# A hybrid conv / state-space / Fourier block on one core: context quarters turned early, C tables turned ahead of B, state tables loaded ahead of the first conv weights

## Chip, cores and metric

One Trainium2 chip, one of its cores. The metric is the device time of the launch in microseconds (us), the median of repeated runs. The profile is of one more execution.

## What is computed

One layer (DEPTH = 1) of a parallel-branch block on 512 latent tokens and 256 context tokens, width 2048, fp32. Cut to what matters here:

```python
mod_x = silu(c) @ w_ada + b_ada          # shift, scale, gate of the latent tokens
mod_c = silu(c_ctx) @ w_ada + b_ada      # the same for the context
h_x = rmsnorm(x, g_pre) * (1 + sc_x) + sh_x
h_c = rmsnorm(ctx, g_pre) * (1 + sc_c) + sh_c
parts_x = split(h_x @ w_in)
u_c = h_c @ w_in[:, U_OFF:U_OFF + W_SSM] # the context is only read by the SSM
# branch B: for both directions
a, bb = zoh(lam, log_dt, b)              # state matrices
cr, ci = scan(u_c, a, bb, None)
xr, xi = scan(u_x, a, bb, h0=last context state)
y = readout(xr, xi, c_re, c_im)
# then conv branch, GLU, Fourier branch, three gated merges, w_out, RMSNorm, residual
```

## The kernel before

Activations are kept transposed: a tile of 128 channels is on the partitions, the tokens are the columns. Every large product is a sum of three fp32r products. ScalarE (ACT) makes the rounded high part of a weight tile (`whi`), VectorE (DVE) or GpSimd (POOL) the remainder (`wlo`); the activations are held as pairs (`hxh`, `hxl` for the latent, `hch`, `hcl` for the context). A unit of weights is 128 x 1024 floats, 512 KB, in one of four slots `wslot`, and is numbered through the program: units 0 to 7 are the first half of U's columns, 8 to 15 the second half (`u_turn`), 16 to 79 the conv turns, and so on. TensorE (PE) counts units done in `w_used`; SyncE (SP) may load unit u when u-3 are done, ACT may convert unit u when u-1 are done.

**Prologue.** SP streams 32 MB of `w_ada` through four `ring` buffers (64 loads of 512 KB, `ada_unit`); PE multiplies each by the two conditioning vectors (`ada(n)`, L631) and frees it (`ada_used`). The model width is taken in four quarters q. For quarter q PE turns the modulation rows into columns (`cols(q)`, L638), DVE makes scale and shift of them (`columns(q)`, L1463), then multiplies and shifts the turned tokens (`modulate`), ACT makes the high part (`high`) and DVE the low part (`low`), and PE multiplies by units 2q and 2q+1: `x_piece(q, r)` for the latent (accumulated in `ac`) and `c_piece(q, r)` for the context (accumulated in banks 0 and 1 of `ss`). Of the latent, 12 of 16 tiles are turned early, unmodulated, into `xT`. The context is turned two tiles at a time by `turn(q, 4)` and `turn(q, 5)` (L665, four 128 x 128 transposes each) into `ss` bank 3, and DVE's `modulate` (L1485) reads it there: so these eight turns stand inside their quarters. Bank 2 of `ss` takes the `ada` products. DVE also makes the state-space parameters between quarters (`zoh`, `chunk_powers`), the latter behind quarter 0 and ahead of `columns(1)`.

**Tables.** The state tables are built once, go to DRAM, and come back in eight blocks b. DVE makes `Bn` (L1544 to L1549) and counts `bb_done`, then powers `Ar`, `Ai` (`ar_done`) and `An` (`an_done`). PE turns `Bn` (`p0_b`) in the first slot inside `u_turn(0)`, behind unit 8, and `craw` (`p0_c`) in the second, behind unit 10. ACT copies the turned B with 16 instructions (`raw_b`) and the turned C with 32 (`raw_c`, in two halves). SP stores all (eight stores, `tab_out`), C last. When all have landed, DVE goes on to `unit_phases` (L1615), since its buffers lie on the stored ones, and SP issues in this order: `tab_load(0)`, `tap_load(0)`, eight small loads of `U`, `u_store(4)`, unit 16, `u_store(5)`, then the four table loads of `state_tables(0)` (`Ah` twice, `Bh` twice; 512 KB each, each DRAM row read again for 16 partitions), unit 17, and on. All are on SP's one queue.

```python
rows_ = src[:, d].rearrange("n g c -> n (g c)")[:, bass.ds(b * (GB * 2 * P), GB * 2 * P)]
rows_ = rows_.unsqueeze(1 - side).to_broadcast([L, H, GB * 2 * P])
```

**Conv turns.** Eight `conv_turn(b)`: PE multiplies eight units (L799, L800, L803: 24 matmuls each), ahead of the third pair it needs `U` and the table product `VT` (L857). DVE first makes `VT` of `Ah` and `Bh` (`state_mults`, `state_adds`, L1651 to L1656), for block 0 waits until POOL has made `wlo` of unit 17, then multiplies `tab` (L1603, L1604), and only then makes `wlo` of unit 18 (L1609): `wlo` of 16 and 17 is POOL's, from 18 on it is DVE's. ACT reads `tab` in `turned_tables(0)` right behind its last copies of `uS`.

```python
st.add(cpy(vcv..., vecs...)); st.wait()
dve.wait_ge(tab_out, 16 * TAB_STORES)
unit_phases()
state_mults(0)
state_adds()
dve.wait_ge(w_lo, U0[1] + 2)
```

Everything from the third turn on (merges, GLU, Fourier, output) is not touched by the change.

## Time and profile before

| | us |
|---|---|
| median of 3 runs | 2051.77 (2050.26 to 2053.57) |
| the profiled execution | 2049.25 |
| its span | 2047.5 |
| PE busy | 1995.4 (97%) |
| DVE busy | 1095.7 (54%) |
| ACT busy | 568.7 (28%) |
| POOL busy | 32.3 (2%) |

The profiled execution lies 2.5 us under the median of the runs. Busy times are of one execution; PEclk is the granted TensorE clock as a share of full speed (1.00 is 2.4 GHz, 0.50 is 1.2 GHz).

### The profile page before, as it was taken

The page shows a single profiled execution, that of the slowest core. Times are in us where ns is not written, and L with a number is a line of the kernel's source. Part 1 is how long each engine was busy: PE and PEld are TensorE (multiplying, and loading weights), DVE is VectorE, ACT ScalarE, POOL GpSimd, SP SyncE. Part 2 cuts the span into 40 slices and gives each one's busy share as a digit, 9 for nine tenths or more (in the row PEclk, how much of TensorE's full clock was granted, in tenths as well). Part 3 has the DMA queues.
Part 4 walks back from the last instruction along what each step waited for, and adds up shares of the span by engine and source line. Part 5 has one row for each costly group of instructions (what it writes and reads, how often), then busy time and mean ns, then how long its engine had stood idle before and what let it go on. Part 6 is the DMA issues. An engine that isn't in the chain of part 4 may idle for free.

```text
span 2047.5 us, 26609 instructions
## 1 busy us (share of the span) xinstructions
PE 1995.4 (97%) x9958; PEld 1628.1 (80%) x9958; DVE 1095.7 (54%) x1647; ACT 568.7 (28%) x795; POOL 32.3 (2%) x16
## 2 busy tenths in 40 slices
PE   4999999999999999999999999999999999999998
PEld 1568788888888888888888888888888888888886
DVE  4547699999998655544334343432433333333325
ACT  5324233333333322222222222222322222222222
POOL 0003200000000000000000000000000000000000
PEclk9999999999999999999999999999999999999999
DMA  9965666656663644443334444443233333334423
GB/s 362 363 203 167 172 152 151 150 147 146 153 152 110 188 128 127 134 138 107 95 94 145 126 132 137 129 132 113 62 97 98 93 103 92 95 100 155 174 99 128
DMA packets 392719, 289.08 MB, mean 141 GB/s; under 512 B 25268, under 2 KB 354460, under 8 KB 390804
## 3 DMA queue, kind: packets, MB, share of 16 engines
q1 hardware_dynamic: 382368, 283.96, 46.4%
q10 hardware_dynamic: 10292, 4.33, 1.4%
q8 instruction: 36, 0.59, 0.1%
q14 instruction: 23, 0.19, 0.0%
HBM read 268.59 MB, written 19.66 MB: 141 GB/s over the span
## 4 chain that ended last, share of the span: by engine, by line
PE 86%; DVE 1%; issue 0%; ACT 0%; DVEq 0%
PE ac L799 25%; PE ac L803 25%; PE ac L800 25%; PE ac L982 1%; PE ac L981 1%; PE ac L980 1%; PE ss L857 1%; PE ss L982 1%; PE ss L981 1%; PE ss L980 1%; DVE Og L1969 0%; PE ss L843 0%; PE ss L880 0%; PE ss L869 0%; PE ss L921 0%; PE ss L884 0%
## 5 line engine op out<-in xcount | busy, mean ns | idle before, releaser
L1609 DVE TENSOR_TENSOR wlo<-wslot,whi 128x1024 fp32r<-128x1024 f32 x309 | 378.4, 1225 | 642.8 <-ACT whi L1016 638.6
L1016 ACT ACTIVATE whi<-wslot 128x1024 fp32r<-128x1024 f32 x327 | 346.9, 1061 | 1264.0 <-PE ac L803 1052.7
L799 PE MATMUL ac<-hxh,whi 128*128 128x512 f32 x1664 | 652.8, 392 | 4.9 <-ACT whi L1016 4.9
L800 PE MATMUL ac<-hxl,whi 128*128 128x512 f32 x1664 | 648.8, 390 | 0.0
L803 PE MATMUL ac<-hxh,wlo 128*128 128x512 f32 x1664 | 411.1, 389 | 1.5 <-DVE wlo L1609 1.5
L799 PEld LDWEIGHTS ac<-hxh,whi 128*128 128x128 f32 x1664 | 313.2, 188 | 73.3 <-ACT whi L1016 5.3
L803 PEld LDWEIGHTS ac<-hxh,wlo 128*128 128x128 f32 x1664 | 312.4, 188 | 66.6 <-DVE wlo L1609 1.9
L800 PEld LDWEIGHTS ac<-hxl,whi 128*128 128x128 f32 x1664 | 313.3, 188 | 63.9
L799 PE MATMUL ac<-bah,whi 128*128 128x512 f32 x384 | 149.5, 389 | 0.0
L800 PE MATMUL ac<-bal,whi 128*128 128x512 f32 x384 | 149.4, 389 | 0.0
L803 PE MATMUL ac<-bah,wlo 128*128 128x512 f32 x384 | 94.8, 389 | 0.0
L799 PEld LDWEIGHTS ac<-bah,whi 128*128 128x128 f32 x384 | 72.1, 188 | 15.0
L803 PEld LDWEIGHTS ac<-bah,wlo 128*128 128x128 f32 x384 | 72.1, 188 | 14.9
L800 PEld LDWEIGHTS ac<-bal,whi 128*128 128x128 f32 x384 | 72.1, 188 | 14.9
L799 PE MATMUL ac<-b2nd,whi 128*128 128x512 f32 x192 | 74.9, 390 | 0.0
L800 PE MATMUL ac<-b2nd,whi 128*128 128x512 f32 x192 | 74.7, 389 | 0.0
L1825 DVE TENSOR_TENSOR gtm<-ac,gsig 128x512 f32<-128x512 f32 x32 | 22.1, 691 | 86.5 <-PE ac L803 86.5
L631 PE MATMUL ss<-ring,cs 128*2 128x512 f32 x256 | 38.0, 675 | 24.1 <-DMA ring<-w_ada 20.8
L1781 DVE SCALAR_TENSOR_TENSOR gacc<-gwt,cs,gacc 128x256 f32<-128x256 f32 x120 | 57.8, 482 | 3.4
L980 PE MATMUL ac<-whi,mhi 128*128 128x512 f32 x128 | 50.2, 392 | 0.0
L982 PE MATMUL ac<-whi,mlo 128*128 128x512 f32 x128 | 49.8, 389 | 0.0
L981 PE MATMUL ss<-wlo,mhi 128*128 128x512 f32 x128 | 49.8, 389 | 0.0
(366 smaller groups left out, 2034.9 us busy)
## 6 DMA issues: line engine op xcount, KB each, us to landing
wslot<-w_in SPq DMA_DIRECT2D x224, 512.0 KB, 3.8
ring<-w_ada SPq DMA_DIRECT2D x64, 512.0 KB, 8.3
gwt<-w_ada SPq DMA_DIRECT2D x128, 128.0 KB, 2.4
wslot<-w_out SPq DMA_DIRECT2D x32, 512.0 KB, 3.6
Ah<-ah_dram SPq DMA_DIRECT2D x16, 512.0 KB
Bh<-bh_dram SPq DMA_DIRECT2D x16, 512.0 KB
wslot<-proj_a SPq DMA_DIRECT2D x16, 512.0 KB, 4.1
wslot<-proj_b SPq DMA_DIRECT2D x16, 512.0 KB, 4.0
```

The source lines that it names most:

```text
L631: last = mm(ss[p:p + 2, 2, :], cs[:, 2 * r + kk, :], ring[n % 4][:, kk, h, :], start=(r == 0), stop=(r == 7))
L799: mm(ac[:, bank, :], w, xh, start=(v == 0 and q == 0), stop=False)
L800: mm(ac[:, bank, :], w, xl, start=False, stop=False)
L803: last = mm(ac[:, bank, :], wlo[:, s, q * 128:(q + 1) * 128], rhs(v * UNIT + q)[0], start=False, stop=(v == nu - 1 and q == UNIT - 1))
L857: last = mm(ss[:, 2 * d + g // 4, (g % 4) * NQ:(g % 4 + 1) * NQ], VT[:, d, g, :], U[:, g, :], start=True, stop=True)
L980: mm(acc[:, t, :], mh, wh, start=(kk == 0), stop=False)
L981: mm(acc[:, t, :], mh, wl, start=False, stop=False)
L982: last = mm(acc[:, t, :], ml, wh, start=False, stop=(kk == KD - 1))
L1016: cp = lambda o, i, scale=1.0: nc.scalar.activation(o, i, ACT.Copy, scale=scale)
L1609: tt(wlo[:, s, :], wslot[:, s, :], whi[:, (U0[k] + j) % 2, :].bitcast(F32), ALU.subtract)\
L1781: stt(gacc[:, :], gwt[:, r % 4, :], cs[:, r, 0:1], gacc[:, :], ALU.mult, ALU.add)\
L1825: tt(o if br == 0 else gtm2[:, :], ac[:, (2 * j + 1) % 4, :], gsig[:, :], ALU.mult)\
```

## The change

`ctx_turn(g)`, g = 0 to 5, turns context tiles 4 to 15 right behind `turn(0, 5)`, into banks 0, 1 and 3 of `ss` in rotation; ACT copies each to `cT` (which lies where `hcl` is), and DVE's `modulate` for q = 1 to 3 reads `cT`. The six turns inside quarters 1 to 3 are gone. `p0_c` takes the first slot in `u_turn(0)` and `p0_b` the second; ACT's copies and SP's stores follow. SP issues `state_tables(0)` right behind `tab_load(0)`; the loads of `U` and `tap_load(0)` go behind unit 17.

```diff
--- before.py
+++ after.py
@@ -206,6 +206,7 @@
     ZN = r("ZN", [128, 7, 2, P])
     assert r.p <= hcl_at
     r = Region(hcl_at)
+    cT = at("cT", [128, KD, TC], r.p)
     hcl = r("hcl", [128, KD, TC], F32R)
     xn = r("xn", [128, TT, D])
     cn = r("cn", [128, CT, D])
@@ -501,9 +502,9 @@
         for n, A in enumerate((Ar, Ai)):
             sp.dma_start(tab_b[:, :, n * 144:(n + 1) * 144], A[:, :, :, :].rearrange("p b e c -> p b (e c)"))\
                 .then_inc(tab_out, 16)
+        late_unit(5)
         sp.wait_ge(p0_cp, 2)
-        sp.dma_start(tab_b[:, :, 544:800], B1[:, :, :].rearrange("p (b c) h -> p b (c h)", c=16)).then_inc(tab_out, 16)
-        late_unit(5)
+        sp.dma_start(tab_b[:, :, 288:544], C1[:, :, :].rearrange("p (b c) h -> p b (c h)", c=16)).then_inc(tab_out, 16)
         sp.wait_ge(an_done, 1)
         for d in range(2):
             places_ = ah_dram[::-1, d] if d == 0 else ah_dram[:, d]
@@ -512,12 +513,10 @@
         late_unit(6)
         late_unit(7)
         sp.wait_ge(p0_cp, 3)
-        sp.dma_start(tab_b[:, :, 288:544], C1[:, :, :].rearrange("p (b c) h -> p b (c h)", c=16)).then_inc(tab_out, 16)
+        sp.dma_start(tab_b[:, :, 544:800], B1[:, :, :].rearrange("p (b c) h -> p b (c h)", c=16)).then_inc(tab_out, 16)
         sp.wait_ge(tab_out, 16 * TAB_STORES)
         tab_load(0)
-        tap_load(0)
-        sp.wait_ge(u_out[0], 16)
-        u_load(0)
+        state_tables(0, [(side, d) for side in range(2) for d in range(2)])
         u_store(4)
 
         for k, (turns, units) in list(enumerate(stream))[1:]:
@@ -545,8 +544,10 @@
                         u_load(i)
                     if k == 1 and j == 4 and not (isinstance(i, int) and i == 0):
                         y_store(i - 1)
-                    if k == 1 and j == 0 and isinstance(i, int) and i == 0:
-                        state_tables(0, [(side, d) for side in range(2) for d in range(2)])
+                    if k == 1 and j == 1 and isinstance(i, int) and i == 0:
+                        sp.wait_ge(u_out[0], 16)
+                        u_load(0)
+                        tap_load(0)
                     if k == 1 and j == 1 and not (isinstance(i, int) and i == 0):
                         tap_load(i)
                     if k == 1 and j == 5 and not (isinstance(i, int) and i == NB - 1):
@@ -647,6 +648,20 @@
                 last = tr(ac[:, k % 4, t * 128:(t + 1) * 128], xn[:, t, k * 128:(k + 1) * 128], ident[:, :])
             last.then_inc(xp_ps, 1)
 
+        def ctx_turn(g):
+            pe.wait_ge(y_done, TT + CT)
+            if g == 2:
+                pe.wait_ge(ht_done, 6)
+            if g > 2:
+                pe.wait_ge(xp_done, EARLY + g - 2)
+            bank = ss[:, (0, 1, 3)[g % 3], :]
+            for kk in range(2):
+                k = 4 + 2 * g + kk
+                for t in range(CT):
+                    last = tr(bank[:, kk * 256 + t * 128:kk * 256 + (t + 1) * 128],
+                              cn[:, t, k * 128:(k + 1) * 128], ident[:, :])
+            last.then_inc(xp_ps, 1)
+
         def turn(q, n):
             if q == 3 or n == 5:
                 pe.wait_ge(ht_done, 6 * q + n)
@@ -710,15 +725,15 @@
 
         def p0_b():
             pe.wait_ge(bb_done, 1)
-            pe.wait_ge(p0_cp, 1)
-            pe.wait_ge(uc_free, 4)
+            pe.wait_ge(p0_cp, 2)
             for h in range(H):
                 last = tr(ss[:, h // 4, (h % 4) * 128:(h % 4 + 1) * 128],
                           Bn[:, h, :, :].rearrange("q r p -> q (r p)"), ident[:, :])
             last.then_inc(p0_ps, 1)
 
         def p0_c():
-            pe.wait_ge(p0_cp, 2)
+            pe.wait_ge(p0_cp, 1)
+            pe.wait_ge(uc_free, 4)
             pe.wait_ge(b_in, 64)
             for h in range(H):
                 last = tr(ss[:, h // 4, (h % 4) * 128:(h % 4 + 1) * 128],
@@ -744,18 +759,20 @@
         turn(0, 4)
         ada(14)
         turn(0, 5)
+        for g in range(6):
+            ctx_turn(g)
         for q in range(3):
             if q:
                 x_piece(q, 0, range(4))
                 ada(8 * q + 12)
                 x_piece(q, 1, range(4))
-                turn(q, 4)
                 ada(8 * q + 13)
                 x_piece(q, 2, range(4))
                 ada(8 * q + 14)
-                turn(q, 5)
                 x_piece(q, 3, range(4))
             ada(8 * q + 15)
+            if q == 0:
+                pe.wait_ge(xp_done, EARLY + 6)
             c_piece(q, 0)
             cols(q + 1)
             if q == 2:
@@ -773,8 +790,6 @@
             for r in range(4):
                 last = x_piece(3, r, (m,))
             last.then_inc(um_ps, 1)
-            if m < 2:
-                turn(3, 4 + m)
         p0_z()
         for r in range(4):
             c_piece(3, r)
@@ -830,7 +845,7 @@
                         last = mm(ac[:, 2 * j + 1, 0:TC], w, hch[:, n, :], **f)
                     last.then_inc(w_used, 1)
                     if i == 0 and v == 0:
-                        (p0_b, p0_c)[j]()
+                        (p0_c, p0_b)[j]()
         for i in range(2):
             u_turn(i)
 
@@ -1077,6 +1092,10 @@
             cp(toks[t], toks[t], small[:, 52 + t:53 + t]).then_inc(y_done, 1)
         high(0, 4)
         high(0, 5)
+        for g in range(6):
+            act.wait_ge(xp_ps, EARLY + g + 1)
+            cp(cT[:, 4 + 2 * g:6 + 2 * g, :], ss[:, (0, 1, 3)[g % 3], :].rearrange("p (k t) -> p k t", k=2))\
+                .then_inc(xp_done, 1)
         for q in range(1, 4):
             rows_cp(q)
             high(q, 0)
@@ -1098,14 +1117,14 @@
             cp(u_of(m)[:, :, 0:NC], places(ss[:, m // 2, (m % 2) * TC:(m % 2 + 1) * TC])).then_inc(uc_free, 1)
 
         def raw_b():
-            act.wait_ge(p0_ps, 2)
+            act.wait_ge(p0_ps, 3)
             for h in range(H):
                 last = cp(B1[:, :, h].rearrange("p (b d g) -> p d b g", b=NB, d=2),
                           ss[:, h // 4, (h % 4) * 128:(h % 4 + 1) * 128].rearrange("p (d b g) -> p d b g", b=NB, d=2))
             last.then_inc(p0_cp, 1)
 
         def raw_c(hs):
-            act.wait_ge(p0_ps, 3)
+            act.wait_ge(p0_ps, 2)
             for h in hs:
                 for ri in range(2):
                     pr = slice(64 * ri, 64 * ri + 64)
@@ -1119,12 +1138,12 @@
             i, j = n // 2, n % 2
             hi(0, i, 2 * j + 2)
             if n == 0:
+                raw_c(range(H // 2))
+            if n == 1:
                 raw_b()
-            if n == 1:
-                raw_c(range(H // 2))
             hi(0, i, 2 * j + 3)
 
-            if n == 1:
+            if n == 0:
                 raw_c(range(H // 2, H))
             act.wait_ge(w_used, U0[0] + 2 * n + 2)
             act.wait_ge(u_out[n], 16)
@@ -1473,8 +1492,10 @@
             k = 4 * q + n
             if n < 4 and k < EARLY:
                 dve.wait_ge(xp_done, k + 1)
+            elif n >= 4 and q:
+                dve.wait_ge(xp_done, EARLY + 2 * (q - 1) + n - 3)
             else:
-                dve.wait_ge(h_ps, 2 * q + (n + 1 if q == 3 else n - 3))
+                dve.wait_ge(h_ps, 2 + n + 1 if q == 3 else n - 3)
             o = htmp[:, n % 3, :]
             if n < 4:
                 x_ = xT[:, k, :] if k < EARLY else ss[:, 3, :]
@@ -1482,7 +1503,7 @@
             else:
                 for kk in range(2):
                     k, w = 4 * q + 2 * (n - 4) + kk, slice(kk * TC, (kk + 1) * TC)
-                    last = ts_(o[:, w], ss[:, 3, w], mod[:, 0, k, 1:2], mod[:, 1, k, 1:2], ALU.mult, ALU.add)
+                    last = ts_(o[:, w], cT[:, k, :] if q else ss[:, 3, w], mod[:, 0, k, 1:2], mod[:, 1, k, 1:2], ALU.mult, ALU.add)
                 last.then_inc(ht_done, 1)
 
         def low(q, n):
```

How the instructions stand now, at three places. PE, behind the last `x_piece` of quarter 0 (`ident` is the identity of a transpose, `cn` the context tokens, `ring` a buffer of `w_ada`), before:

```order
L665 MATMUL ss<-ident,cn 128x128 [waits y_done,ht_done]
L665 MATMUL ss<-ident,cn 128x128 x3
L631 MATMUL ss<-ring_95,cs 2x512 [waits ada_in3]
L631 MATMUL ss<-ring_95,cs 2x512 x3
L692 MATMUL ss<-hch,zrow 128x512 [waits h_done]
L692 MATMUL ss<-hch,zrow 128x512
```

and now:

```order
L661 MATMUL ss<-ident,cn 128x128 [waits xp_done,y_done]
L661 MATMUL ss<-ident,cn 128x128 x3
L632 MATMUL ss<-ring_95,cs 2x512 [waits ada_in3]
L632 MATMUL ss<-ring_95,cs 2x512 x3
L707 MATMUL ss<-hch,zrow 128x512 [waits h_done,xp_done]
L707 MATMUL ss<-hch,zrow 128x512
```

The first two rows are the last of the six context turns; five such pairs stand ahead of it, of which the third waits for `ht_done` and the fourth and fifth for a copy by ACT (`xp_done`), as the sixth does. The first instruction of `c_piece(0, 0)` now waits for the last copy.

PE, the first slot of `u_turn(0)`, between the products of units 8 and 9, before:

```order
L829 MATMUL ac<-hxh,wlo 128x512
L830 MATMUL ac<-hch,wlo 128x256
L716 MATMUL ss<-ident,Bn 128x128 [waits uc_free,p0_cp,bb_done]
L716 MATMUL ss<-ident,Bn 128x128 x15
L820 MATMUL ac<-hxh,whi 128x512 [waits w_hi]
```

and now:

```order
L844 MATMUL ac<-hxh,wlo 128x512
L845 MATMUL ac<-hch,wlo 128x256
L739 MATMUL ss<-ident,craw 128x128 [waits b_in,uc_free,p0_cp]
L739 MATMUL ss<-ident,craw 128x128 x15
L835 MATMUL ac<-hxh,whi 128x512 [waits w_hi]
```

The turn of B, and with it the wait for `bb_done`, has moved to the second slot, behind unit 10, where C's turn was; there it waits for `p0_cp` 2, which is ACT's copy of all of C.

SP's queue, from the last table store on, before:

```order
L515 DMA tab_dram<-C_109 1024x1x256 [waits p0_cp]
L441 DMA tab<-tab_dram 128x544 [waits tab_out]
L448 DMA tab<-tab_dram 128x256
L470 DMA U<-u_dram 16x8x96 [waits u_out0]
L470 DMA U<-u_dram 16x8x96 x7
L433 DMA u_dram<-uS 128x768 [waits ac_free0]
L536 DMA wslot<-w_in 128x8x128 [waits w_used]
L433 DMA u_dram<-uS 128x768 [waits ac_free2]
L460 DMA Ah<-ah_dram 128x1x1024 x2
L460 DMA Bh<-bh_dram 128x1x1024 x2
L536 DMA wslot<-w_in 128x8x128 [waits w_used] x2
```

and now:

```order
L516 DMA tab_dram<-B_108 1024x1x256 [waits p0_cp]
L442 DMA tab<-tab_dram 128x544 [waits tab_out]
L461 DMA Ah<-ah_dram 128x1x1024 x2
L461 DMA Bh<-bh_dram 128x1x1024 x2
L434 DMA u_dram<-uS 128x768 [waits ac_free0]
L535 DMA wslot<-w_in 128x8x128 [waits w_used]
L434 DMA u_dram<-uS 128x768 [waits ac_free2]
L535 DMA wslot<-w_in 128x8x128 [waits w_used]
L471 DMA U<-u_dram 16x8x96 [waits u_out0]
L471 DMA U<-u_dram 16x8x96 x7
L449 DMA tab<-tab_dram 128x256
L535 DMA wslot<-w_in 128x8x128 [waits w_used]
```

The four table loads stand ahead of units 16 and 17, and the nine loads of `U` and the taps stand behind unit 17 and ahead of unit 18.

## Rows read from the trace of the kernel before

**Rows 1.** The waits of PE over the whole span: total us, times, longest.

```profile
PE ss L631 <- DMA ring<-w_ada: 20.8, 5, 15.5
PE ac L799 <- ACT whi L1016: 4.9, 1, 4.9
PE ss L631 <- DVE vmod L1463: 3.3, 2, 3.0
...
PE ac L803 <- DVE wlo L1609: 1.5, 1, 1.5
```

**Rows 2.** Windows: length, busy us of PE, PEld, DVE, ACT, POOL, PEclk, DMA share, GB/s.

```profile
53.00:54.00 1.00, 1.00 (x4) 0.72 (x3) 0.68 (x2) 1.00 (x2) 0.00 (x0) 0.50 1.05 385
76.00:80.00 4.00, 1.04 (x11) 0.18 (x9) 3.55 (x17) 0.00 (x0) 0.00 (x0) 1.00 0.93 342
228.00:234.00 6.00, 6.00 (x37) 5.22 (x36) 3.28 (x9) 0.00 (x0) 1.24 (x1) 1.00 0.52 131
246.00:247.00 1.00, 1.00 (x4) 0.81 (x3) 0.96 (x2) 0.97 (x2) 1.00 (x1) 0.50 1.19 333
262.00:300.00 38.00, 38.00 (x251) 31.57 (x251) 37.43 (x59) 14.83 (x26) 0.00 (x0) 1.00 0.70 152
```

**Rows 3.** PE's timeline in quarters 0, 1 and 3: start, duration, what.

```profile
68.25 0.66 PE L665 MATMUL ss<-ident,cn 128*128 128x128 f32 x4
68.83 1.04 PE L631 MATMUL ss<-ring,cs 128*2 128x512 f32 x8
...
71.62 0.73 PE L692 MATMUL ss<-hch,zrow 1*128 1x512 f32 x2
...
79.24 1.04 PE L631 MATMUL ss<-ring,cs 128*2 128x512 f32 x8 [2.96 <-DVE vmod L1463]
...
92.10 1.07 PE L682 MATMUL ac<-hxh,wlo 128*128 128x512 f32 x4
93.01 0.60 PE L665 MATMUL ss<-ident,cn 128*128 128x128 f32 x4
93.54 1.04 PE L631 MATMUL ss<-ring,cs 128*2 128x512 f32 x8
```

**Rows 4.** DVE and ACT around the context turns and the tables: start, duration, what.

```profile
71.32 0.99 DVE L1485 TENSOR_SCALAR htmp<-ss,vmod 128x256 f32<-128x256 f32 x2
...
41.92 1.57 ACT L1016 ACTIVATE xT<-ac 128x512 f32<-128x512 f32 x3
...
182.02 1.06 ACT L1016 ACTIVATE whi<-wslot 128x1024 fp32r<-128x1024 f32 x1 [4.51 <-PE ac L830]
...
201.61 6.38 ACT L1016 ACTIVATE C<-ss 64x128 f32<-64x128 f32 x16
```

**Rows 5.** PE's timeline from the Bn wait to the third pair of conv units.

```profile
171.67 1.97 PE L716 MATMUL ss<-ident,Bn 128*128 128x128 f32 x16 [2.45 <-DVE Bn L1549]
...
233.93 0.40 PE L799 MATMUL ac<-hxh,whi 128*128 128x512 f32 x1
...
259.25 0.39 PE L799 MATMUL ac<-hxh,whi 128*128 128x512 f32 x1
...
264.70 0.47 PE L857 MATMUL ss<-U,VT 128*128 128x96 f32 x3
```

**Rows 6.** DVE and ACT where they wait for tables and weights.

```profile
212.94 0.11 DVE L1615 MEMSET Elo<- 128x64 f32 x1 [17.17 <-DMA tab_dram<-C]
...
241.79 2.29 DVE L1651 TENSOR_TENSOR VT<-Ah,Bh 128x2048 f32<-128x2048 f32 x1 [10.40 <-DMA Bh<-bh_dram]
...
243.37 1.06 ACT L1016 ACTIVATE whi<-wslot 128x1024 fp32r<-128x1024 f32 x1 [16.61 <-DMA wslot<-w_in]
```

**Rows 7.** SP's queue: start and time that the issues took.

```profile
208.01 0.57 SPq L515 DMA_DIRECT2D tab_dram<-C  x1
219.47 1.45 SPq L460 DMA_DIRECT2D Ah<-ah_dram  x2
...
222.39 12.20 SPq L536 DMA_DIRECT2D wslot<-w_in  x2
```

## The prediction

> **What bounds the kernel.** I read the totals first, then PE's waits, then windows, then the timelines of the two stretches that the change touches. PE is busy 97% of the span, and its waits add up to some 40 us, half of them for the first `w_ada` loads, which the change leaves alone [rows 1]. From 262 us on PE is busy all the time, at full clock, with DVE close behind (37.4 of 38 us) [rows 2]; I take it that all from there on only shifts with the moment at which PE gets there. So the question is how much sooner PE reaches its first state product (L857, 264.70) [rows 5].
>
> **Term 1, the context turns.** A turn in a row of turns takes PE 0.58 us (68.25 to the next start at 68.83) [rows 3]. The six new ones start where `ada(15)` stood, 0.97 ahead of 71.62, behind `turn(0, 5)`. The first two run to 71.8. The third waits until DVE has read bank 3, 71.32 + 0.99 = 72.3 [rows 4]. ACT then makes the high part of the same tile until 72.95 and copies at 0.52 to 0.55 us each (three in 1.57) [rows 4], six until 76.2. The last three turns are paced by these copies and end at 75.2, `ada(15)` at 76.2. So `c_piece(0, 0)`, which started at 71.62, starts at 76.2: 4.6 us later [rows 3]. Of that PE had 2.96 us idle before `ada(16)` at 79.24, waiting for `columns(1)` on DVE, which is behind `chunk_powers` there and is not delayed by the turns [rows 3]. With `cols(1)` 4.6 us later, DVE has its columns at 79.7 and PE is at `ada(16)` at 80.85: **+1.6**. If the copies cost nothing this is about 0, if the cover were gone 4.6; I take 1.6, the sum of the rows.
>
> Removed are four turns in quarters 1 and 2. Such a turn holds `ada` back from 93.01 to 93.54 [rows 3]; some 0.1 of it would pass in any case until the next start, so I count 0.42 each, **-1.7**. Two go from the stretch of quarter 3, where PE is short of nothing after 144.2, at 0.36 each: **-0.7**. ACT's six copies and DVE's reads, now from SBUF, lie where both engines are two thirds idle. The `w_ada` queue is refilled 4.6 us late once, by `ada(15)`; the ring has three loads ahead and PE waits for none of them after 51 us, so I cost this at nothing. Sum of term 1: -0.8.
>
> **Term 2, B behind C.** PE waits 2.45 us for `Bn` ahead of the first slot [rows 5]. `craw` is loaded in time, and the 16 transposes take the same. In the second slot, 18 us later, `Bn` is ready. What is late next there is `p0_cp` 2, ACT's copy of C: its first half (6.38 us) starts when PE has turned C, its second right behind the conversion of unit 11. That conversion waited for PE at 182.02 and took 1.06, so the copy ends at 182.02 + 1.06 + 6.38 = 189.5 [rows 4] on the old clock, where PE arrives at 190.25: 0.7 us to spare. **-2.45**, and nothing comes back.
>
> **Term 3, tables and weights.** Unit 16 starts at 233.93 and L857 at 264.70, with four units between [rows 5]. One unit without a wait takes 5.45 (259.25 to 264.70), four 21.8; so 30.8 - 21.8 = 9.0 us are lost: 4.93 waiting for unit 17, 1.5 for DVE's `wlo` of unit 18 [rows 1], and the rest to the granted clock, 0.50 when PE comes back [rows 2]. The chain: the last table store lands at 212.9, the tables are issued from 219.47, `Bh` is there at 241.7, and unit 17, issued at 222.39 behind them, at 243.3 [rows 6, 7]. DVE cannot start `VT` before, and so makes `wlo` of unit 18 late.
>
> What becomes of each. B's copy takes less than C's second half and ends near 193; the last store is now issued behind unit 15 on SP, which waits for PE's unit 11 (200.5 before, 197.2 now): at 198.2. Alone the store took 4.9 us (208.01 to 212.9) [rows 6, 7]; behind two weight loads and the stores of `An` I take 8.5, until 206.7, 6 us sooner than before. The tables are issued at 207.1 to 210. How long they take has two bounds: 16.0 us, their 2.1 MB at 131 GB/s, the rate at which the queue ran while little but they were in it [rows 2], and 22.2, their time from issue to use before (219.47 to 241.7), with the loads of `U`, two stores and unit 16 ahead of them. Now only `tab` (272 KB) is ahead, so I take 17.5 with 0.8 for `tab`: 225.4.
>
> Unit 16 now stands behind them. `u_store(4)` and its own 512 KB, at the 385 GB/s of the prologue [rows 2], add 2.4 and the completion about 1: 228.8, and with the conversion 229.9. PE wants it at 233.93 - 3.25 = 230.7: 0.8 us to spare. Unit 17 follows by 2.4 us, its turn comes 5.5 later. `VT` takes DVE 9 us, until 235; DVE then waits for POOL's `wlo` of unit 17, at most 4 us behind a conversion that ends at 231.9; its products of `tab` (5.2) and `wlo` of unit 18 end near 243, and PE wants that one at 245.2. `U` and the taps, behind unit 17, are due at 252.6. So nothing is short, by one or two us each: **-8.9**.
>
> Behind unit 16 stands a rule. The DMA share is 0.52 while the tables run [rows 2]: half the 16 engines carry them. The Trainium skill says so too (DMA: Bandwidth & Descriptors, "Rules for kernel authors": an outermost dimension of c < 16, such as a broadcast's, keeps a DMA on at most c engines; here it is L = 8), and its section "Queues, rings and completion order" that each engine takes its descriptors in the order of the ring. That speaks against this change: whatever is issued behind the tables waits for the eight slow engines, and now that is unit 16, not 17.
>
> **Sum**: -0.8 - 2.45 - 8.9 = -12.1. The profiled execution took 2049.25, 2.5 less than the median of the runs; it would take 2037.1, and the median goes from 2051.77 to **2039.7**.
>
> **Rivals.**
> A, the forecast: all three terms, 2037.5 to 2041.5. Chance 0.62.
> B, the tables still take 22.2 us. They are there at 229.3, unit 16 converted at 233.8: PE waits 3 us, and if the clock falls again another 2 are lost. -7 to -9.5, middle 2043.3. For it: the margin of 0.8. Against: the queue ahead is empty. 0.17.
> C, the clock falls in the row of context turns. After the thin `ada` products and transposes before 47 us and a wait, the granted clock was 0.50 until 54, some 6.5 us [rows 2]; PE's work there at half speed costs up to 3.3: 2043.0. Against: at 76 to 80 PE idled 2.96 us and the clock stayed at 1.00 [rows 2]. 0.11. The Trainium skill (TensorE: Matmul & The Clock Gate, "Part 4: PE-mode transpose") says that transposes do not count as activity for the clock; by that rule C would be the likelier.
> D, the change does not do what it says: the tables' time does not move with their issue, or unit 16 takes over unit 17's wait in full. Then terms 1 and 2 alone are left: 2048.5. 0.07.
> E, slower. The `w_ada` queue is full at 385 GB/s ahead of 76 us, and its share falls there only since the ring is full [rows 2]; refilled 4.6 us late, it starves PE at each `ada` from 16 on, PE waits each time, and the clock stays at 0.50. 4.6 us plus half of 24 us of work is 16.6, against 12.1 gained: 2056.3. It decides once more than 15 us run at half speed. Against: no wait for `ring` after 51 us. 0.03.
>
> **Numbers.** 0.2%, 4.1 us, is about what a measurement of this kernel can tell from no change. A, B and C are faster (0.90), D is the same (0.07), E slower (0.03). The range holds A, B's bound of -7 and C, and leaves out D and E: 2037 to 2045.
>
> **What would show it.** Right: `c_piece(0, 0)` near 76 and `ada(16)` near 81 with no wait for `vmod`; no wait at the first slot, and none for `p0_cp` at the second; the last table store landing near 207; `VT` starting near 226; unit 16 starting on PE near 230.7 with no wait for `whi`, clock 1.00 through to L857 near 252.6. Wrong: PE waiting for `whi` of unit 16, or the clock at 0.50 at 76 to 82 or after 230; a wait for `ring` after 80; or a new wait of PE behind 262, which would mean that DVE or the loads do not follow the earlier start.

## The result, and the profile after

| | before | after |
|---|---|---|
| median of the runs, us | 2051.02 (4 runs, 2049.53 to 2053.57) | 2037.19 (4 runs, 2035.90 to 2037.82) |
| ratio to before | | 0.9929, 95% interval 0.9913 to 0.9944 |
| the profiled execution, us | 2049.25 | 2037.82 |
| its span | 2047.5 | 2036.0 |
| start of L857 (first state product) | 264.70 | 252.96 |
| span behind that start | 1782.8 | 1783.0 |

The kernel is faster by 13.8 us between the medians, 0.7%. The stretch behind L857 is as long as it was within 0.3 us, so what was gained lies in the first 265 us. These are waits of PE in the changed kernel, over the whole span (total us, times, longest), in the form of [rows 1]:

```profile
PE ss L632 <- DMA ring<-w_ada: 20.4, 5, 14.9
...
PE ac L697 <- DVE wlo L1519: 2.1, 1, 2.1
...
PE ss L661 <- DVE htmp L1506: 0.9, 1, 0.9
...
PE ss L661 <- ACT cT L1031: 0.5, 1, 0.5
PE ss L632 <- DVE vmod L1482: 0.3, 1, 0.3
```

The waits for `whi` of unit 17 (4.9), for `wlo` of unit 18 (1.5) and for `Bn` (2.45) are gone, and `vmod` fell from 3.0 (the longest) to 0.3. New are 0.9 and 0.5 inside the row of context turns (`htmp` and `cT`). The windows, with the columns of [rows 2] (length; busy us of PE, PEld, DVE, ACT, POOL; granted clock; DMA share; GB/s), show what the clock did:

```profile
53.00:54.00 1.00, 1.00 (x4) 0.74 (x3) 1.00 (x2) 1.00 (x1) 0.00 (x0) 0.50 1.05 387
69.00:77.00 8.00, 6.43 (x52) 3.59 (x48) 5.20 (x16) 4.18 (x8) 0.00 (x0) 1.00 1.05 385
80.00:84.00 4.00, 4.00 (x33) 3.00 (x33) 2.32 (x8) 2.21 (x3) 0.00 (x0) 1.00 0.51 180
...
246.00:247.00 1.00, 1.00 (x6) 0.84 (x5) 1.00 (x2) 0.00 (x0) 0.00 (x0) 1.00 0.87 186
254.00:300.00 46.00, 46.00 (x304) 38.11 (x304) 43.30 (x63) 17.20 (x30) 0.00 (x0) 1.00 0.66 150
```

The clock is at 1.00 through the row of turns, and at 246 us, where it was 0.50. In the window from 254 to 300 us PE is never idle, with DVE close behind it (43.3 of 46 us) as before.

PE's timeline (start, duration, what, idle time before), against [rows 3] and [rows 5]:

```profile
71.64 1.04 PE L661 MATMUL ss<-ident,cn 128*128 128x128 f32 x8
73.53 0.63 PE L661 MATMUL ss<-ident,cn 128*128 128x128 f32 x4 [0.86 <-DVE htmp L1506]
74.68 1.60 PE L661 MATMUL ss<-ident,cn 128*128 128x128 f32 x12 [0.52 <-ACT cT L1031]
76.21 1.04 PE L632 MATMUL ss<-ring,cs 128*2 128x512 f32 x8
77.18 0.73 PE L707 MATMUL ss<-hch,zrow 1*128 1x512 f32 x2
...
81.74 1.04 PE L632 MATMUL ss<-ring,cs 128*2 128x512 f32 x8
...
168.98 1.91 PE L739 MATMUL ss<-ident,craw 128*128 128x128 f32 x16
170.65 0.48 PE L835 MATMUL ac<-hxh,whi 128*128 128x512 f32 x1
...
231.16 0.40 PE L814 MATMUL ac<-hxh,whi 128*128 128x512 f32 x1
...
252.96 1.25 PE L872 MATMUL ss<-U,VT 128*128 128x96 f32 x10
```

The four units between 231.16 and 252.96 take 21.80 us, exactly four times the undisturbed 5.45. SP's queue (start, time that the issues took), against [rows 7]:

```profile
200.07 1.47 SPq L516 DMA_DIRECT2D tab_dram<-B  x1
208.21 0.34 SPq L442 DMA_DIRECT2D tab<-tab_dram  x1
208.59 1.45 SPq L461 DMA_DIRECT2D Ah<-ah_dram  x2
210.08 1.97 SPq L461 DMA_DIRECT2D Bh<-bh_dram  x2
...
212.59 0.43 SPq L535 DMA_DIRECT2D wslot<-w_in  x1
213.07 8.69 SPq L434 DMA_DIRECT2D u_dram<-uS  x1
221.80 0.43 SPq L535 DMA_DIRECT2D wslot<-w_in  x1
```

DVE and ACT at the places of [rows 6], and the copies of C and B:

```profile
170.93 6.47 ACT L1031 ACTIVATE C<-ss 64x128 f32<-64x128 f32 x16 [0.68 <-PE ss L739]
180.34 6.45 ACT L1031 ACTIVATE C<-ss 64x128 f32<-64x128 f32 x16
...
189.43 3.77 ACT L1031 ACTIVATE B<-ss 128x128 f32<-128x128 f32 x16 [0.66 <-PE ss L730]
...
226.57 1.06 ACT L1031 ACTIVATE whi<-wslot 128x1024 fp32r<-128x1024 f32 x1 [9.99 <-DMA wslot<-w_in]
...
208.38 0.11 DVE L1636 MEMSET Elo<- 128x64 f32 x1 [12.04 <-DMA tab_dram<-B]
...
225.28 2.29 DVE L1672 TENSOR_TENSOR VT<-Ah,Bh 128x2048 f32<-128x2048 f32 x1
```

The last table store landed at 208.4 (before 212.9). `VT` starts at 225.28 instead of 241.79 and carries no idle time any more: the tables were there by then, and DVE came from `unit_phases` without a pause. Unit 16 is converted at 227.63, 3.5 us before PE starts it at 231.16.

### The profile page after: what moved, and what is told of

It is laid out like the page before. It is cut to its first block, busy times and chain, and to the rows that moved or that the text cites. A ratio compares the mean times of both kernels' runs of the same rounds, so it can differ in the third digit from the quotient of the medians.

```text
span 2036.0 us, 26614 instructions
## 1 busy us (share of the span) xinstructions
PE 1993.9 (98%) x9958; PEld 1626.2 (80%) x9958; DVE 1094.9 (54%) x1647; ACT 571.7 (28%) x801; POOL 32.0 (2%) x16
## 4 chain that ended last, share of the span: by engine, by line
PE 94%; DVE 2%; DMA 2%; ACT 1%; issue 1%; SPq 0%; DVEq 0%; ACTq 0%
PE ac L814 25%; PE ac L815 24%; PE ac L818 24%; PE ac L995 1%; PE ac L997 1%; PE ac L996 1%; PE ss L872 1%; PE ss L632 1%; PE ss L997 1%; PE ss L995 1%; PE ss L996 1%; PE ac L693 1%; PE ac L844 1%; PE ac L694 1%; PE ac L836 1%; PE ac L697 1%
## 5 line engine op out<-in xcount | busy, mean ns | idle before, releaser
L632 PE MATMUL ss<-ring,cs 128*2 128x512 f32 x256 | 38.7, 686 | 20.7 <-DMA ring<-w_ada 20.4
```

What stands on the lines that cost most here:

```text
L632: last = mm(ss[p:p + 2, 2, :], cs[:, 2 * r + kk, :], ring[n % 4][:, kk, h, :], start=(r == 0), stop=(r == 7))
```

## The span cut at four places

The sum of the prediction can be laid beside the two profiled executions if PE's timeline is cut where the change acts: at `ada(10)`, the first conditioning product behind the early latent turns (ahead of every edit), at the start of unit 8, of unit 9 and of unit 16, and at L857. All further comparisons use these stretches. The first is ahead of every edit: it took between 54.8 and 56.6 us in all the profiles here, whatever the kernel, so its +1.09 is no work of the change.

| stretch, us | before | after | difference | forecast |
|---|---|---|---|---|
| start to `ada(10)` | 55.52 | 56.61 | +1.09 | 0 |
| to unit 8 (term 1) | 105.23 | 104.06 | -1.17 | -0.8 |
| to unit 9 (term 2) | 12.65 | 9.98 | -2.67 | -2.45 |
| to unit 16 | 60.53 | 60.51 | 0 | 0 |
| to L857 (term 3) | 30.77 | 21.80 | -8.97 | -8.9 |
| to the end | 1782.80 | 1783.04 | +0.24 | 0 |
| sum | 2047.5 | 2036.0 | -11.5 | -12.1 |

Between these two executions each term is right within 0.4 us. But the medians differ by 13.8, and by 15.0 when both were run once more (below), more than these terms add up to, and the experiments below were chosen to find where the rest is, and to separate the terms.

## Experiments

### Four kernels with parts of the change

**e1_turns**, term 1 alone. `ctx_turn` and `cT` in, the six turns out of their quarters, tables and SP's order as before:

```diff
+        for g in range(6):
+            ctx_turn(g)
...
-                turn(q, 4)
...
-                turn(q, 5)
```

> The context turns alone (cT), tables and SP's order as before. Theory: the 4.6 us that c_piece(0, 0) is late are paid for by the wait of PE for columns(1) (2.96) and by the six turns that are gone later (2.4), so -0.8 to -1.2 us; ada(16) later by 1.4 to 1.6, unit 8 earlier by 0.8 to 1.2. Rival 1: the turns and ACT's copies are paid in full, +2 us. Rival 2: the clock falls at 72 to 80 us, +2 to +3.

**e2_cfirst**, term 2 alone, with the semaphore counts that go with it:

```diff
-                        (p0_b, p0_c)[j]()
+                        (p0_c, p0_b)[j]()
```

> C turned, copied and stored ahead of B alone; SP's order of tables and weights as before. Theory (the tables' issue and the order both matter): -2.5 us at the first slot of u_turn, no wait at the second; the last table store is issued 6 to 7 us sooner, the tables are there about 5 us sooner, and unit 17's wait of 4.9 us shrinks by 2 to 3 and may spare the clock: -5 to -8 us in all. Rival (only the order of SP's queue matters for the later stretch): -2.5 us.

**e3_order**, SP's order of term 3 alone, with the tables' stores as before (C last):

```diff
-        tap_load(0)
-        sp.wait_ge(u_out[0], 16)
-        u_load(0)
+        state_tables(0, [(side, d) for side in range(2) for d in range(2)])
...
-                    if k == 1 and j == 0 and isinstance(i, int) and i == 0:
-                        state_tables(0, [(side, d) for side in range(2) for d in range(2)])
+                    if k == 1 and j == 1 and isinstance(i, int) and i == 0:
+                        sp.wait_ge(u_out[0], 16)
+                        u_load(0)
+                        tap_load(0)
```

> Only the order of SP's queue changed: state tables ahead of units 16 and 17, U and the taps behind unit 17; the last table store lands at 212.9 us as before. Theory: tables there at about 231, unit 16 about 3.4 us later at 234.4 and converted at 235.5, where PE wants it at 233.9: PE waits 1.5 to 2.5 us for unit 16, none for unit 17 and none for wlo of unit 18: -6 to -7.5 us. Rival 1 (the order alone gives all): -8.9. Rival 2 (unit 16 takes over unit 17's wait): within 1 us of before.

**e4_no_order**, the changed kernel with the diff of e3_order undone: terms 1 and 2.

> The whole change but for the order of SP's queue (tables behind U, unit 16 and two stores, as before). Theory: terms 1 and 2 (-3.3 to -3.8 us) and the earlier last store's part, together -6 to -9 us; unit 17 still waited for, by 2 to 4 us. Rival (the last store's time is worth nothing without the order): -3.5 us.

Measured, each against 24 runs of before (median 2051.39):

| kernel | median (runs) | ratio, 95% | difference |
|---|---|---|---|
| e1_turns | 2048.09 (12) | 0.9985, 0.9973 to 0.9997 | -3.1 |
| e2_cfirst | 2046.17 (12) | 0.9971, 0.9958 to 0.9985 | -6.0 |
| e3_order | 2041.52 (7) | 0.9955, 0.9938 to 0.9972 | -9.2 |
| e4_no_order | 2043.00 (6) | 0.9955, 0.9937 to 0.9973 | -9.2 |

The differences are those of the ratio, applied to 2051.4. Terms 1 and 2, forecast at -0.8 and -2.45, are worth -3.1 and -6.0 in the runs, and -9.2 together. SP's order alone, e3_order, brings what was forecast for term 3. The two halves, -9.2 and -9.2, add up to more than the whole change brought (13.8 to 15.8 us, by medians or by ratio); each is known to 3.5 us or so, and the runs don't tell whether the halves overlap. Here is PE's timeline of e3_order and then of e4_no_order, at the conv unit where each waits:

```profile
236.83 0.47 PE L799 MATMUL ac<-hxh,whi 128*128 128x512 f32 x1 [0.33 <-ACT whi L1016]
```

```profile
240.91 0.80 PE L814 MATMUL ac<-hxh,whi 128*128 128x512 f32 x1 [4.68 <-ACT whi L1031]
```

With tables first, unit 16 was 0.33 us late (1.5 to 2.5 were expected), and it took 21.89 us from there to L857. Yet the last store landed no sooner against PE than in before: 21.2 us ahead of PE's arrival at unit 16 (215.3 and 236.5), in before 21.0 (212.9 and 233.9). With terms 1 and 2 and the old order the store landed 23.1 us ahead of that arrival (207.5 and 230.6), but PE waits 4.68 us for unit 17, much as in before (4.93), and the stretch is 29.25. So it is the order, and not the earlier landing of the last store, that brings term 3.

### The two kernels once more

**before_again** and **after_again** are the two kernels unchanged, on a second chip.

> The kernel before once more, for its profile. Theory: each wait of PE of 2 to 3 us in the prologue (columns(1) near 77, wlo near 143, Bn near 170) is followed by a fall of the granted clock in some executions and not in others, 1.0 to 1.6 us each; so the stretch from ada(10) to unit 8 takes 105.2 us as in the first profile, or 1.5 or 3 more. Rival: it is 105.2 within 0.3 and the other profiles were longer for another reason.

> The changed kernel once more. Theory: ratio near 0.993; ada(10) to unit 8 takes 104.1 us within 0.3 unless the clock falls behind the wait near 143 (then 105.6); the runs spread less than those of before, as two of the three waits are gone.

Measured: after_again 2036.33 (6 runs, 2035.93 to 2036.82), ratio to before 0.9923 (0.9906 to 0.9940). Before took 2051.31 there (17 runs), from 2044.75 to 2056.52. The kernel before spreads over 12 us in its 17 runs, the one after over 0.9 in its 6 (and over 1.9 in the first 4). The execution of before_again took 2046.33. Two further executions of the unchanged kernel on a third chip:

> The kernel before a third time, for its profile; its runs lie between 2044.8 and 2057. Theory: what differs between executions are the falls of the granted clock behind its waits and the time from the last table store to VT (26.3 and 28.9 us in the first two profiles), so ada(10) to unit 8 is 105.2 plus 0, 1.5 or 3, unit 8 to unit 16 is 73.2 plus 0 or 1.4, unit 16 to L857 is 28 to 33. Rival: the difference lies elsewhere, behind 265 us.

> The kernel before a fourth time, for its profile. Theory and rival as for the third: the three stretches ahead of L857 carry what differs from the first profile, and the stretch behind it is 1782.6 to 1783.2 us again.

They took 2052.07 and 2051.99, where the median of 19 runs of before was 2053.93. So there are four profiled executions of the same kernel, which are cut as above; with them the waits of PE that differ and the stretches at a granted clock of 0.50 behind 57 us:

| | before | again | third | fourth |
|---|---|---|---|---|
| `ada(10)` to unit 8 | 105.23 | 105.27 | 105.22 | 109.49 |
| to unit 9 | 12.65 | 12.62 | 16.36 | 12.58 |
| to unit 16 | 60.53 | 60.53 | 60.54 | 60.54 |
| to L857 | 30.77 | 28.30 | 29.77 | 28.73 |
| wait for `Bn` | 2.45 | 2.42 | 4.64 | 2.27 |
| clock at 0.50 | 241-249 | 241-249 | 173-178, 245-253 | 78-86, 147-151, 246-253 |

The window 78 to 82 us, of before and then of before_fourth, with the columns of [rows 2]:

```profile
78.00:82.00 4.00, 2.76 (x24) 1.70 (x28) 2.98 (x11) 1.73 (x3) 0.00 (x0) 1.00 0.59 188
```

```profile
78.00:82.00 4.00, 2.27 (x10) 0.57 (x11) 3.10 (x13) 1.51 (x2) 0.00 (x0) 0.62 0.52 192
```

The PE timeline of the fourth shows the cause: the same wait for `columns(1)`, 2.97 us (2.96 in the first), and behind it the eight `ada` matmuls took 1.89 us where they took 1.04 [rows 3].

```profile
79.72 1.89 PE L631 MATMUL ss<-ring,cs 128*2 128x512 f32 x8 [2.97 <-DVE vmod L1463]
```

The third exceeded what was expected behind `Bn` (3.7 us instead of at most 1.4), the fourth ahead of unit 8 (4.3 instead of at most 3). At `Bn` PE's timeline of before_third shows 3.50 us for the sixteen transposes that took 1.97 in [rows 5]:

```profile
174.09 3.50 PE L716 MATMUL ss<-ident,Bn 128*128 128x128 f32 x16 [4.64 <-DVE Bn L1549]
```

So a wait of 2 to 3 us leaves the clock at 1.00 in one execution and takes it to 0.50 in another. A fall came with `columns(1)` (fourth, e2_cfirst, e3_order), with the wait for `wlo` near 143 us (fourth, e3_order, e8_u_first), with `Bn` (third, e1_turns, e5_chunk), with unit 17 (all four, and e1_turns, e2_cfirst, e4_no_order, e5_chunk) and, in e1_turns, with `wlo` of unit 18 (1.97 us). The eight waits of 3.0 to 5.7 us between 57 us and L857 in all these profiles each had one, and two of them are the `Bn` waits of 4.64 and 4.65: the dear case there is the longer wait and the half clock together. The two falls of the fourth cost 109.49 - 105.24 = 4.25 us. At `Bn` the third lost 16.36 - 12.63 = 3.7: 2.2 of it a longer wait, 1.5 the clock.

The longer wait has a cause of its own. These are DVE's steps of the chain that makes `Bn`, all of one form, in before and then in before_third:

```profile
160.99 1.97 DVE L1546 TENSOR_TENSOR btmp<-ZN,braw 128x1024 f32<-128x1024 f32 x1
...
166.35 4.01 DVE L1548 TENSOR_TENSOR btmp<-ZN,braw 128x1024 f32<-128x1024 f32 x1
170.39 1.22 DVE L1549 TENSOR_TENSOR Bn<-Bn,btmp 128x1024 f32<-128x1024 f32 x1
```

```profile
161.20 4.17 DVE L1546 TENSOR_TENSOR btmp<-ZN,braw 128x1024 f32<-128x1024 f32 x1
...
168.75 1.92 DVE L1548 TENSOR_TENSOR btmp<-ZN,braw 128x1024 f32<-128x1024 f32 x1
170.71 3.33 DVE L1549 TENSOR_TENSOR Bn<-Bn,btmp 128x1024 f32<-128x1024 f32 x1
```

A step takes 1.2 to 2.0 us, or some 2.1 longer. In before two of the six are long (L1547 and L1548), in the third three (L1546, L1547 and L1549). POOL makes `wlo` in the same stretch, in before and then in before_third:

```profile
159.34 9.23 POOL L607 TENSOR_TENSOR wlo<-wslot,whi 128x1024 fp32r<-128x1024 f32 x2 [157.86 <-ACT whi L1016]
170.40 3.45 POOL L607 TENSOR_TENSOR wlo<-wslot,whi 128x1024 fp32r<-128x1024 f32 x1 [1.82 <-ACT whi L1016]
```

```profile
170.62 2.34 POOL L607 TENSOR_TENSOR wlo<-wslot,whi 128x1024 fp32r<-128x1024 f32 x1 [2.99 <-ACT whi L1016]
```

Such a POOL instruction alone takes 2.4 us, here 3.45 and more. Look at who starts first at the last step. In before DVE's L1549 starts at 170.39 and POOL at 170.40: DVE takes 1.22, POOL 3.45. In the third POOL starts at 170.62 and DVE at 170.71: POOL takes 2.34, DVE 3.33. It is so in all fourteen profiles of this case, with DVE ahead in six and POOL in eight: the one that starts first, by 0.01 to 0.18 us, takes its 1.2 or 2.4, the other 3.3 to 3.5, about the sum of both. That one of the two waits while the other works is what this says. The steps before do not decide it: e3_order has the third's 4.16 and 3.31 at L1546 and L1547, but DVE is first at L1549, and PE's wait is 2.36. No run took POOL out of the stretch to confirm it.

The kernel after has one wait of over 1.2 us left between 57 and 253 us, 2.12 for `wlo` ahead of 145.02, and e8_u_first shows that the clock can fall there too. Its two profiles agree in every stretch within 0.03 us (104.06 and 104.03, 9.98 and 9.98, 60.51 and 60.52, 21.80 and 21.79), and the clock is at 1.00 from 57 us on in both.

### The wait for columns(1) by itself

**e5_chunk** is before with `chunk_powers` moved, so that `columns(1)` comes 4 us sooner and PE's longest wait for `vmod` goes from 3.0 to 0.3:

```diff
+            if q == 1:
+                chunk_powers()
             if q == 0:
                 token_scale
...
-            if q == 0:
-                chunk_powers()
```

> The kernel before, with DVE's chunk_powers moved from ahead of columns(1) to behind lo_first(3), and nothing else. Theory (the change's first part gains because PE no longer waits for columns(1), and the clock no longer falls behind that wait): -3.0 us where the clock had stayed, -4.5 where it had fallen, so -3 to -4.5 in the median, more than the turns' -1.2 to -3.1. Rival (the wait near 77 is hidden by the w_ada loads anyway): PE waits for ring instead, 0 to -1 us.

Measured: 2046.75 (12 runs), ratio 0.9978 (0.9965 to 0.9992), -4.6 us. In its profile `ada(10)` to unit 8 takes 102.16, 3.1 less than in before. That the runs show 1.5 more fits the half clock that such a wait sometimes brings, but the interval (1.6 to 7.2 us) does not tell 4.6 from 3.1. The profiled execution shows only 1.2 of gain in all (2048.05 against 2049.25), since it fell into the dear case at `Bn`:

```profile
173.00:178.00 5.00, 5.00 (x22) 4.52 (x21) 4.90 (x11) 3.17 (x15) 0.00 (x0) 0.58 0.81 190
```

It waited 4.65 us for `Bn`, and unit 9 followed 16.44 us behind unit 8. From these two profiles alone the edit would have been priced at a quarter of what the runs show.

**e6_best** takes parts 2 and 3 of the change and this edit in place of part 1: the context stays turned inside its quarters, and `chunk_powers` goes behind `lo_first(3)`.

> Parts 2 and 3 of the change (C ahead of B, tables ahead of the weights), the context turned inside its quarters as before, and chunk_powers behind lo_first(3). Theory: 1.8 us faster than the changed kernel (no 4.6 us of early turns and copies; the six turns inside the quarters cost 2.4 again): about 2035.5, ratio 0.992; ada(10) to unit 8 takes 102.3 us. Rival (the first part is worth as much as this): the same as the changed kernel within 0.5 us.

Measured: 2035.15 (6 runs, 2034.69 to 2035.86), ratio to before 0.9918 (0.9901 to 0.9935). That beats both kernels: after_again on the same chip took 2036.33, and no run of it was under 2035.93. `ada(10)` to unit 8 takes 102.22 against 104.03, the other stretches are alike to 0.01 us. 1.8 us in the profile, 1.2 between the medians. The early turns are thus a roundabout way to hide the wait for `columns(1)`: they fill it with six turns, and moving what delayed `columns(1)` does without them.

### Two orders undone in the changed kernel

**e8_u_first**, the changed kernel with the taps and `U` ahead of the tables again:

```diff
         tab_load(0)
+        tap_load(0)
+        sp.wait_ge(u_out[0], 16)
+        u_load(0)
         state_tables(0, [(side, d) for side in range(2) for d in range(2)])
```

> The changed kernel with the loads of U and the taps ahead of the tables again; the tables still ahead of units 16 and 17. Theory: the tables are issued 4.5 us later and take as long or longer behind the small loads: VT 21 to 24 us behind the last store in place of 17, unit 16 converted 3 to 5 us too late; PE waits 3 to 5 us for it: +3 to +6 us, about 2040 to 2042. Rival (what matters is only that tables stand ahead of the weights): the same as the changed kernel.

Measured: 2044.58 (10 runs, 2039.04 to 2046.49), ratio 0.9956 (0.9941 to 0.9970). These runs and those of e9_b_first were made on the third chip, where before took 2053.93, 2.6 more than on the second, and are to be set against that: e8_u_first gains 9.0 to 9.4 us there, some 6 less than the changed kernel on the second. Its SP queue, and DVE where it waits for the tables:

```profile
208.46 4.64 SPq L471 DMA_DIRECT2D U<-u_dram  x8
213.14 1.45 SPq L461 DMA_DIRECT2D Ah<-ah_dram  x2
```

```profile
228.97 2.29 DVE L1671 TENSOR_TENSOR VT<-Ah,Bh 128x2048 f32<-128x2048 f32 x1 [3.98 <-DMA Bh<-bh_dram]
```

The tables are issued 4.55 us later than in after, and are there 15.8 us from their issue (213.14 to 228.97). Unit 16 then comes late, and PE waits 1.52 us for it:

```profile
232.61 0.47 PE L813 MATMUL ac<-hxh,whi 128*128 128x512 f32 x1 [1.52 <-ACT whi L1030]
```

In that execution all of 1.5 was lost, and 1.6 to a fall at 144 to 149 us. Three of the ten runs lie at 2039.0 to 2040.3, seven at 2043.9 to 2046.5, none between. The profile is of one of the three. What the other seven lost is not shown: a fall of the clock behind unit 16 is possible, but no wait under 1.97 us had one in these profiles.

**e9_b_first**, the changed kernel with part 2 undone, B turned and stored ahead of C:

```diff
-                        (p0_c, p0_b)[j]()
+                        (p0_b, p0_c)[j]()
```

> The changed kernel with B turned, copied and stored ahead of C as before (part 2 undone). Theory: PE waits 2.4 us for Bn ahead of the first slot, with a fall of the clock behind it in some executions (1.4 us); the last store is C's again and later by some 5 us against PE, so unit 16 is waited for by 0 to 1 us: +2.5 to +5 us, about 2039 to 2041. Rival (C's store then lets the tables come too late, PE waits in full for unit 16): +7 us.

Measured: 2042.18 (10 runs, 2038.57 to 2049.02), ratio 0.9953 (0.9939 to 0.9967). The profile is of the fastest run, 2038.57: PE waits 2.4 us for `Bn`, unit 8 to 9 takes 12.60, the clock holds, and everything else is as in after, 21.79 us to L857 included, although the last store landed nearer to PE's arrival at unit 16 (211.3 and 232.3, 21.0 us; 22.8 in after). So the wait's own price is 2.6 us. The runs say 3 to 6: against before on its own chip e9_b_first gained 9.7 by the ratio and 11.8 by the medians, after_again 15.8 and 15.0 on its own. What makes the rest in its slower runs no profile shows; the dear case at `Bn`, 3.7 us, is the candidate.

## Where the prediction held, and the step that failed

**Direction and mechanism** were right. What forecast A says happened: the waits for `Bn`, unit 17 and `wlo` of unit 18 went, and nothing of their size took their place. The time did not come out as forecast: 2037.19 is 2.5 us under the predicted 2039.7, under A's own 2037.5 to 2041.5, and at the very edge of the stated 2037 to 2045; by the ratio, 0.9929 of 2051.02, it is 2036.5 and outside of both.

**The step that failed** is the last of the sum: "it would take 2037.1, and the median goes from 2051.77 to 2039.7". The 2.5 us between the profiled execution of before and the median of its runs were carried over to the changed kernel as if they were a fixed offset. They are not. In the changed kernel the profiled execution lay 0.6 us above the median of its runs the first time, 0.2 under it the second, and the runs spread over 1.9 and 0.9 us where before spreads over 12. The offset went with the waits, and so it belonged to the gain: 13.8 and 15.0 us by the medians instead of 12.1.

How the offset was made up is shown in part. The profiles show what an execution can pay beyond the first one of before: 3.7 us at `Bn`, 1.5 to 4.3 for the half clock ahead of unit 8. But their average does not hold it all: from `ada(10)` to L857 before takes 209.18, 206.72, 211.89 and 211.34, on average 209.8, and after 196.35 and 196.32. That is 13.4 us against 12.8 in the one pair, 0.6 more and not 2.5. None of the four lies above 2052.1, where the runs of before go up to 2057, and what those pay for is open.

The sizes of the terms are off in the same direction: term 1 was priced at -0.8 and measured -1.2 in the profiles and -3.1 in the runs, term 2 at -2.45, measured -2.7 and -6.0. The intervals of these two results are some 2.5 us to either side: that of term 2 excludes the forecast price, that of term 1 does not. Not all of the -6.0 is the wait for `Bn`: the profile of e2_cfirst also takes 27.44 us from unit 16 to L857, where the four of before take 28.3 to 30.8.

**Term 1.** `c_piece(0, 0)` started 77.18 - 56.61 = 20.57 us behind `ada(10)`, where before it was 16.10: 4.5 later, 4.6 forecast. `ada(16)` came 25.13 behind against 23.72, +1.4 (forecast +1.6), and the wait for `vmod` shrank to 0.3. The pacing by ACT's copies shows as 0.52 us of wait, that by DVE's read of bank 3 as 0.86. The removed turns gave 2.6 instead of 2.4.

**Rival C** did not come. Its case rested on the clock falling in the row of turns; PE idled there 1.4 us in two pieces and the window 69 to 77 is at 1.00, as in e1_turns, e4_no_order, after_again, e8_u_first and e9_b_first. The Trainium skill (TensorE: Matmul & The Clock Gate, "Part 4: PE-mode transpose") says that transposes do not count as activity for the clock; no row of this case shows that here, and a row of six turns among products did not bring the clock down. But the evidence brought against the rival, "at 76 to 80 PE idled 2.96 us and the clock stayed at 1.00", was one throw of a die: before_fourth fell at the same place, behind the same wait.

**Term 2** went as written, with nothing coming back: the copy of C ended at 186.79 (180.34 + 6.45), and `p0_b` started at 187.49 without a wait: the 0.7 us to spare were there.

**Term 3.** Its size was right at 8.97. Two of its steps were off and cancelled. The last store landed at 208.4, not 206.7: it was issued at 200.07, not 198.2, of which 1.1 is the later `ada(10)` of this execution, and took 8.3 where 8.5 was assumed. And the tables and unit 16 took less: 19.4 us from the issue of `tab` to unit 16 converted (208.21 to 227.63), where 22.8 were forecast (207.1 to 229.9). The margin for unit 16 was so 3.5 us, not 0.8. In e9_b_first and e3_order, where the store landed 1.8 and 1.6 us nearer to PE's arrival, it took 19.9 and 21.5 us from the issue of `tab` to unit 16 converted; the one had 1.3 us left, the other lost 0.3. One part of the sum can be seen by itself: unit 16 was there 2.4 and 2.6 us behind the tables where both were waited for (e8_u_first 228.97 to 231.41, e3_order 233.00 to 235.63), where the forecast had 3.4, "the completion about 1" included. `VT` started at 225.28 (forecast 226) but for another reason: DVE had its phases to finish, which take 16.9 us from the landing of the last store. Two kernels show the tables' own time, since DVE waited for them there: 15.8 us in e8_u_first, just under the lower bound of 16.0, and 17.5 in e3_order (215.54 to 233.00), the value that the forecast took.

```profile
233.00 2.29 DVE L1651 TENSOR_TENSOR VT<-Ah,Bh 128x2048 f32<-128x2048 f32 x1 [1.44 <-DMA Bh<-bh_dram]
```

So the 131 GB/s of [rows 2] is near their rate. With the old order the four profiles of before took 22.3, 19.7, 21.0 and 20.4 us: the forecast's upper bound was the longest of them, and 2 to 7 us in it go to what was issued around the tables. That this is unit 16 ahead of them is likely, and no run shows it by itself.

The rule that spoke against the change (the Trainium skill, DMA: Bandwidth & Descriptors, "Rules for kernel authors" and "Queues, rings and completion order") agrees with the trace as far as it goes: unit 16 does wait behind the tables, since ACT idles 9.99 us for it. It just was not late. Rival B needed 22 us for the tables; in the four kernels with the tables first (after, e3_order, e6_best, e9_b_first) `VT` started 16.3 to 17.7 us behind the landing of the last store.

**Rivals D and E** did not come: `VT` moved by 16.5 us with the order, and no wait for `ring` appeared behind 57 us.

**Left open:** what the dearest executions of before pay for; why a wait brings the clock down in one execution and not in the next; what separates the two groups of e8_u_first; and whether the tables on all 16 DMA engines would free U's place, which wasn't tried.

## What to carry to other kernels

Price a wait of PE by the runs, not by one profile: the wait itself is in every execution, the half clock behind it only in some, and the spread of the runs (12 us here, 0.9 without most of the waits) hints at how much of it there is. When a profiled execution lies under the median, do not carry the difference over to the changed kernel as it is: ask whether the waits that you remove make it, and widen the range on that side. And when a wait can be hidden by moving work into it, look first at what the waited-for engine does just ahead: moving `chunk_powers` was worth 1 to 2 us more than filling the gap.

## What was new about the hardware

- With a PE wait of 2 to 3 us the granted clock fell to 0.50 in some executions and not in others, at the same instruction. A fall cost about 1.5 us at `Bn` (16 transposes 3.50 instead of 1.97 us), 1.5 at `columns(1)` in e2_cfirst (106.73 instead of 105.23), 1.6 near 144 us in e8_u_first (105.66 instead of 104.04), and 4.25 for two in before_fourth. At unit 17 (4.9 us in [rows 1]) it fell in all four profiles of before.
- DVE steps of one form (128x1024, f32) in the chain of `Bn` took 1.2 to 2.0 us or 3.3 to 4.2, and POOL's `wlo` beside them 3.3 to 4.6 where alone it takes 2.4. At the last step, in all fourteen profiles, the engine that started first, by as little as 0.01 us, took its short time and the other waited it out. When that was POOL, and PE was waiting for `Bn` (before_third, e5_chunk), PE's wait was 4.65 us instead of 2.4.
- A DMA issue behind the four table loads held SP's queue for 8.69 us (`u_store(5)` at 213.07), and in before two such issues took 12.20 [rows 7]. The profile names nothing that they waited for; that it was the queue's own room is inferred.
